# Moving the loads of the transposed h from SyncE's DMA queue to GpSimd's in a two-layer hybrid encoder

## What is computed

```
x = x + 0.5 * swiglu(rmsnorm(x, ffn1_norm), ffn1_w_in, ffn1_w_out)      # D_FF = 2816
h = rmsnorm(x, mix_norm);  p = h @ w_mix_in
out_a = spatial gating over 128-position chunks of p's first 1024 columns
out_b = windowed attention, 8 q heads and 2 kv heads of 64, relative bias rel_bias[bucket], sink
x = x + concat(out_a, out_b) @ w_mix_out
x = x + 0.5 * swiglu(rmsnorm(x, ffn2_norm), ffn2_w_in, ffn2_w_out)
```

## Time and profile before

| | us |
|---|---|
| median of 3 runs | 897.25 |
| lowest, highest | 891.78, 897.42 |
| the profiled execution | 896.2 |
| its span, first to last instruction | 894.4 |

### The profile page before, as it was taken

How to read it: one execution, slowest core, us unless ns; L and a number is a source line. 1 busy time by engine, 2 the same in 40 slices (tenths; PEclk the granted TensorE clock), 3 DMA queues, 4 the chain that set the end, 5 groups by cost and what they waited for, 6 DMA issues and landing times.

```text
span 894.4 us, 11077 instructions
## 1 busy us (share of the span) xinstructions
PE 875.7 (98%) x4118; PEld 715.9 (80%) x4118; DVE 709.5 (79%) x857; ACT 507.0 (57%) x554; POOL 63.8 (7%) x123
## 2 busy tenths in 40 slices
PE   9998999899999999999999999998999999999998
PEld 8886878788788778788887788887877887788887
DVE  6796868667978798878687889775889788989773
ACT  6555637447956466466354664562678573655550
POOL 4200000012101000000010000000111010000000
PEclk9998999999999999999999999999999999999999
DMA  9758677894086858666857587687822878667651
GB/s 316 260 177 263 210 251 247 208 300 157 1 264 210 279 184 286 221 195 248 275 166 242 187 297 248 193 274 236 232 93 71 259 238 273 207 234 227 220 200 48
DMA packets 138469, 194.51 MB, mean 217 GB/s; under 512 B 9796, under 2 KB 94600, under 8 KB 138416
## 3 DMA queue, kind: packets, MB, share of 16 engines
q1 hardware_dynamic: 136432, 189.17, 65.2%
q0 software_dynamic: 1808, 4.49, 2.5%
q10 hardware_dynamic: 176, 0.14, 0.0%
HBM read 179.61 MB, written 14.16 MB: 217 GB/s over the span
## 4 chain that ended last, share of the span: by engine, by line
PE 66%; DVE 17%; DMA 8%; ACT 4%; issue 2%; SPq 2%; ACTq 0%; DVEq 0%
DVE w_lo L1176 7%; PE U L1729 6%; PE U L1732 6%; PE U L1730 6%; PE C L1729 5%; PE C L1730 5%; PE C L1732 5%; PE TR L1729 5%; PE TR L1732 5%; PE TR L1730 5%; PE D L1729 4%; PE D L1730 4%; PE D L1732 4%; DMA gv<-h_rows 4%; DMA h_rows<-qs 3%
## 5 line engine op out<-in xcount | busy, mean ns | idle before, releaser
L1176 DVE TENSOR_TENSOR w_lo<-raw,w_hi 128x2048 fp32r<-128x2048 f32 (+1 forms) x182 | 401.8, 2236 | 47.7 <-ACT w_hi L793 47.2
L793 ACT ACTIVATE w_hi<-raw 128x2048 fp32r<-128x2048 f32 (+1 forms) x178 | 331.7, 1892 | 139.1 <-DVE raw L1201 59.5
L1729 PE MATMUL U<-w_hi,xT 128*128 128x512 f32 (+1 forms) x384 | 147.7, 385 | 0.3 <-DVE xT L1354 0.3
L1730 PE MATMUL U<-w_lo,xT 128*128 128x512 f32 (+1 forms) x384 | 146.2, 381 | 0.0
L1732 PE MATMUL U<-w_hi,xT 128*128 128x512 f32 (+1 forms) x384 | 146.1, 380 | 0.0
L1729 PE MATMUL TR<-w_hi,xT 128*128 128x512 f32 x224 | 87.4, 390 | 0.0
L1732 PE MATMUL TR<-w_hi,xT 128*128 128x512 f32 x224 | 87.2, 389 | 0.0
L1730 PE MATMUL TR<-w_lo,xT 128*128 128x512 f32 x224 | 87.1, 389 | 0.0
L1729 PEld LDWEIGHTS U<-w_hi,xT 128*128 128x128 f32 x384 | 72.2, 188 | 15.6 <-issue 0.8
L1729 PE MATMUL C<-w_hi,hT_hi 128*128 128x512 f32 x176 | 71.7, 408 | 12.3 <-DVE hT_lo L1268 12.3
L1732 PEld LDWEIGHTS U<-w_hi,xT 128*128 128x128 f32 x384 | 72.2, 188 | 13.9
(11 more groups left out here) (210 smaller groups left out, 1238.8 us busy)
## 6 DMA issues: line engine op xcount, KB each, us to landing
raw<-in_ffn_w_in_dram SPq DMA_DIRECT2D x168, 512.0 KB, 5.3
raw<-in_ffn_w_out_dram SPq DMA_DIRECT2D x88, 512.0 KB, 5.5
raw<-in_w_mix_in_dram SPq DMA_DIRECT2D x28, 512.0 KB, 9.5
raw<-in_w_mix_out_dram SPq DMA_DIRECT2D x16, 512.0 KB, 4.4
h_rows<-qs SPq DMA_DIRECT2D x31, 256.0 KB, 2.3
gv<-h_rows SPq DMA_DIRECT2D x124, 64.0 KB, 3.8
raw<-in_ffn_w_in_dram SPq DMA_DIRECT2D x16, 256.0 KB, 4.9
xc<-bias_rows POOLq DMA_DIRECT2D x16, 192.0 KB, 7.4
```

What stands on the lines that cost most here:

```text
L793: return act.activation(w_hi[:, slot_of(u), cols], raw[:, raw_of(u), cols], ACT.Copy)
L1176: return dve.tensor_tensor(w_lo[:, slot_of(u), cols], raw[:, raw_of(u), cols], w_hi[:, slot_of(u), cols].bitcast(F32), ALU.subtract)
L1729: pe.matmul(out_, x_hi, w_hi[:, slot, c], start=start, stop=False, skip_group_check=reopened)
L1730: pe.matmul(out_, x_hi, w_lo[:, slot, c], start=False, stop=False, skip_group_check=reopened)
```

## The change

- `load_h` and `load_g` are issued by GpSimd, with the same waits, data and semaphores. SyncE issues only the stores and the weights, and no longer waits for the stores' landing.
- On GpSimd's queue, `load_h(0, 1)` and `load_h(0, 2)` stand ahead of the store of the bias rows, which now follows unit (0, "out", 2). In layer 1 the loads for chunks 0, 1 and 2 stand ahead of the `ws` loads. All other loads of a layer's first stage stand behind `ws`, `sgain` and `sinks` and ahead of the `bias` loads; those of the second stage behind that layer's last rsqrt for the mixing part.
- The `bias` loads follow (s, "out", 9), three times (s, "out", 7), four times (s, "out", 8).
- In stages 1 to 3 SyncE issues `load_block(s, 3, "B12")` directly behind `store_h(s, 0)`, and `load_out(s, 1)` behind it; before, `load_out(s, 1)` came first and B12 behind the loads of h.
- ScalarE's `round_h(s, 2)` comes ahead of `made(5, 1)`.

```diff
@@ ffn_weights (SyncE), stages 1 to 3
                     store_h(s, 0)
+                    load_block(s, 3, "B12")
                     load_out(s, 1)
-                    load_h(s, 0)
-                    load_block(s, 3, "B12")
                     store_h(s, 1)
                     load_in(s, 5, 0)
-                    load_h(s, 1)
                     load_block(s, 3, "B22")
                     load_out(s, 2)
                     load_in(s, 5, 1)
                     store_h(s, 2)
-                    load_h(s, 2)
...
@@ gpsimd
+            def load_h(s, c):
+                n = TRIP_ORDER[s, c]
+                pool.wait_ge(h_stored, 16 * n)
+                if n > 1:
+                    pool.wait_ge(hT_lo_done, n_h_rest(n - 1))
+                for g in range(4):
+                    src = ...
+                    pool.dma_start(h_cols[32 * g:32 * g + 32, :]..., src).then_inc(h_loaded, 16)
...
-            pool.wait_ge(units_used, n_used((0, "out", 1)))
+            load_h(0, 1)
+            load_h(0, 2)
+            pool.wait_ge(units_used, n_used((0, "out", 2)))
             pool.dma_start(bias_rows, ...)
             for L in range(DEPTH):
                 if L == 0:
                     pool.wait_ge(bias_stored, 16)
+                else:
+                    load_h(s, 0)
+                    load_h(s, 1)
+                    load_h(s, 2)
                 for j, u in enumerate([(s, "sum", 3, "B11"), (s, "sum", 3, "T2"), (s, "in", 5, 0), (s, "in", 6, 0)]):
                     ...
+                load_h(s, 5)
+                load_g(s, 3)
+                load_h(s, 3)
+                load_h(s, 6)
+                load_h(s, 9)
+                load_g(s, 7)
+                load_h(s, 7)
-                for i, u in enumerate([(s, "sum", 7, "B22"), (s, "sum", 7, "B21"), (s, "sum", 7, "T4"), (s, "in", 10, 0),
-                                       (s, "in", 10, 1), (s, "out", 9), (s, "out", 7), (s, "out", 8)]):
+                for i, u in enumerate([(s, "out", 9), *[(s, "out", 7)] * 3, *[(s, "out", 8)] * 4]):
                     ...
                 inverse_rms(L, 2, 1)
+                for c in (0, 1, 2, 5):
+                    load_h(s + 1, c)
+                load_g(s + 1, 3)
+                for c in (3, 6, 9):
+                    load_h(s + 1, c)
+                load_g(s + 1, 7)
+                load_h(s + 1, 7)
@@ scalar
+                round_h(s, 2)
                 made(5, 1)
-                round_h(s, 2)
```

More of the change, by code:

```diff
@@ L552, in store_h @@
                 sp.dma_start(h_rows[n % 2], h_turns).then_inc(h_stored, 16)
[L554 to L563, removed]
             def store_g(s, c):
@@ L571, in store_g @@
                 sp.dma_start(g_rows, g_turns).then_inc(g_stored, 16)
[L573 to L579, removed]
             def trip_of_x(n):
@@ L640, in ffn_weights @@
                 load_block(s, 7, "B12")
-                load_h(s, 5)
                 store_g(s, 3)
@@ L644, in ffn_weights @@
                 store_h(s, 3)
-                load_g(s, 3)
                 load_block(s, 7, "B22")
-                load_h(s, 3)
                 load_in(s, 9, 0)
@@ L652, in ffn_weights @@
                 load_block(s, 7, "B21")
-                load_h(s, 6)
                 load_in(s, 10, 0)
@@ L660, in ffn_weights @@
                 load_out(s, 10)
-                load_h(s, 9)
                 store_g(s, 7)
                 store_h(s, 7)
-                load_g(s, 7)
-                load_h(s, 7)
                 if after is not None:
@@ L730, in norm, with load_g @@
                       groups).then_inc(rstd_done, 1)
+            def load_h(s, c):
[4 more added lines that the diff above has]
+                for g in range(4):
+                    src = bass.AP(h_rows.tensor, TRIP_ORDER[s, c] % 2 * P * 2 * FC + g * P, [[2 * FC, 32], [32 * 2 * FC, 4], [1, P]])
+                    pool.dma_start(h_cols[32 * g:32 * g + 32, :].rearrange("p (i n) -> p i n", i=4), src
+                                 ).then_inc(h_loaded, 16)
+            def load_g(s, c):
+                pool.wait_ge(g_stored, 16 * TRIP_B_ORDER[s, c])
+                for g in range(4):
+                    src = bass.AP(g_rows.tensor, g * P, [[2 * FC, 32], [32 * 2 * FC, 4], [1, P]])
+                    pool.dma_start(g_cols[32 * g:32 * g + 32, :].rearrange("p (i n) -> p i n", i=4), src
+                                 ).then_inc(g_loaded, 16)
             inverse_rms(0, 0, 0)
```

## The result

The changed kernel takes 928.3 us (median of 4 executions, 925.9 to 933.1), the kernel before 897.3 (4, 891.8 to 899.1): ratio 1.036, 95% interval 1.030 to 1.042. It is slower by 31 us where the prediction had 5 us less, and it lies outside the range of 883 to 904. The profiled execution of after took 925.9 (span 924.1, mean granted clock 0.985; before 894.4 and 0.994).

A forecast was written before the change was run, and what follows sets the result against it. TensorE, busy 98% of the span, bounds the kernel, so only its few gaps can be won. Terms -6.3 - 7.2 - 2.2 - 1.1 + 8.0 + 0 + 3.5 = -5.3 us: 896.2 to 890.9, median 892.0; range 883 to 904.

The forecast's parts named there:

- Chunk 2 of stage 0, and chunk 9: Gaps and clock: -6.3 us at chunk 2 of stage 0, -7.2 us at chunk 9 of stages 0 and 2.
- Chunk 5 of stages 0 and 2, the new wait: h(5)'s loads wait behind the last ws load on GpSimd: stall 2.6 us, +8.0 us for both stages.
- Chunk 0 of stages 1 to 3: TensorE's gap 1.5 us, three times 4.6 us as before, so 0; bounds -3.5 and +13.
- L4: Time from the fourth load's issue to landing: about 4.0 us at chunk 0, about 5.8 us at pair 7.
- first rival: GpSimd's loads pass the weights: pair 7 costs 0, chunk 0 -3.5 more; total -13.3 us, median 884; chance 0.15.
- landings of 7 behind weights: GpSimd's h loads were to land in 4 to 6 us behind weights; 3 or 7 would make the prediction wrong.
- Pair 7: SyncE, let go, puts mix weights ahead of the loads: stall 1.75 us, +3.5 us for stages 0 and 2; others 0.
- Chunk 2 of stages 1 to 3 and pair 3: Rounding first gives -2.2 us at chunk 2; GpSimd issuing g's loads gives -1.1 us at pair 3, stage 1.
- Held back B12: At chunk 0 of stages 1 to 3, SyncE's loads of h held back B12 before; no size given.
- the second: Under a saturated queue four GpSimd loads land late, L4 6 at chunk 0: +12.9 us, median 910; chance 0.12.
- The third: TensorE's gaps close but VectorE and ScalarE show them elsewhere: gains halved (+3), median 900; chance 0.12.
- The fourth: VectorE starves descriptors: each of 31 trips 2.25 us later, some 11 in the open: +20 us, median 917; chance 0.03.

The follow-up runs named there:

- Experiment 1: The run of e1_others: kernel before with only the bias-row, bias-load and rounding edits: 880.1 us, ratio 0.980.
- e5_order: Changed kernel with only the order out(1), then B12 restored as in the kernel before, nothing held: 930.3 us, ratio 1.037.
- f_pool_issued: f_pool, but SyncE issues B12 only when GpSimd has issued the four loads of h(0): 892.8 us, ratio 0.997.
- f_pool_landed: f_pool, but SyncE issues B12 only when the four loads of h(0) have landed: 880.3 us, ratio 0.983.
- f_act: f_pool, but ScalarE issues the loads of h(0) on its own queue, ahead of round_h(0): 898.2 us, ratio 1.004.
- e1_others: Kernel before with only the bias rows and bias loads moved and round_h(s, 2) first; all h and g loads stay on SyncE: 880.1 us, ratio 0.980.
- g_landed: Changed kernel with h(5)'s loads ahead of the last ws load and SyncE stopping at each old place until loads have landed: 881.6 us, ratio 0.984.
- f_pool: e1_others, but GpSimd issues the loads of h(0) in stages 1 to 3 and SyncE goes on without a wait: 897.7 us, ratio 1.001.
- g_best: e1_others with load_h(s, 0) ahead of load_out(s, 1) and load_h(s, 3) ahead of load_block(s, 7, B22), all on SyncE: 877.5 us, ratio 0.979.

## Why the prediction was wrong

- **Chunk 2 of stage 0, and chunk 9: right.** -6.3 and -7.2 against -6.5 and -6.8. Experiment 1 shows that they didn't need the new queue.
- **Chunk 5 of stages 0 and 2, the new wait: right.** +8.0 against +9.0 in the trace and +9.9 alone; the gaps were 3.78 and 3.33 us where 2.6 was worked out.
- **Chunk 0 of stages 1 to 3: the step that failed.** The relation (gap = L4 - 2.46) held within 0.3 us: 6.66 gives 4.2 where 4.5 was seen, 7.67 gives 5.2 where 5.4 was. What failed is the term L4: 4.0, worked out from "some 1.2 MB ahead", against 6.7 to 7.7. The bytes were too few: SyncE's queue moved 1.97 MB between the fourth issue and the landing. But the right bytes would not have saved it: e5_order moved 1.30 MB there and landed at 6.8 us. The sentence that led to it was "So a GpSimd load stands behind what SyncE has issued". From a stretch in which GpSimd's queue moved nothing I took a single line in order of issue, in which a load pays only for what stands ahead. The window right behind it, in which SyncE's queue had 58.5% and GpSimd's 53.8%, showed the two sharing; the prediction saw this under its first rival and left it out of the sum. f_pool_issued and f_pool_landed differ only in whether B12 runs beside the loads, and by 12.5 us. The prediction's own sign of being wrong, landings of 7 behind weights, came.
- **Pair 7: half right.** That SyncE let go would put weights beside the loads was seen, for stages 0 and 2; it was sized by the weights ahead (L4 5.8, +3.5) and set to nothing in stage 1. The landings took 7.4, 6.6 and 7.4 us in stages 0, 1 and 2. It costs 12.1 in the trace and 12.8 alone.
- **Chunk 2 of stages 1 to 3 and pair 3:** the small gains came in stages 1 and 2 of chunk 2 (-0.8 and -0.7); chunk 2 of stage 3 and pair 3 lost 5.3 and 2.9. The prediction gave h(3) over 1 us of slack; its loads landed 6.9 and 7.2 us behind the fourth issue in stages 1 and 3, where they had taken 4.6 in stage 1. At chunk 2 of stage 3 the loads landed after 5.6 us beside weights, behind GpSimd's pause of 1.35 us.
- **Held back B12:** the prediction noted that before, the loads "held back B12", and gave this no value. B12 behind the loads in the same queue went with a landing of 3.6 us; about as much of it issued around them from another queue, with 5.9 (f_pool_issued).

Of the rivals, the second, with 0.12, had the right place and the fall of the clock behind it. It spoke of GpSimd loads under a saturated queue; the condition is right (with B12 held away the landing fell to 2.8 to 3.7 us), but f_act shows that they needn't be GpSimd's, and its L4 of 6 was still short. Its 910 left out stage 1 of pair 7. The first, that GpSimd's loads pass the weights, is wrong in the sum: they do get packets in among them, and still land last. The third, that the gains show up again as waits elsewhere, is refuted by e1_others: the terms that it times were worth 15.7 us in the sum and gave 17. The fourth, a trip 2.25 us later for each of 31, finds no such cost in g_landed, where the 39 trips' issues lie beside a VectorE busy 81%. In after, GpSimd's 124 issues of h took (shortest, median, longest in ns):
```profile
L709 POOL DMA_DIRECT2D gv<-h_rows x124: 548/548/675, 45.5 to 898.9; - x124
```
The Trainium skill, SBUF — State Buffer, section SBUF: two separate sides, by which VectorE's two-port instructions hold off GpSimd's writing of descriptors, spoke against the change; this row shows at most 0.13 us of it on one issue. The pause of 1.35 us between two issues isn't in the row; VectorE was making low parts of weights through all of it, and whether that held GpSimd no run tells.

On packets, the Trainium skill, DMA: Bandwidth & Descriptors, section Queues, rings and completion order, says that a DMA engine takes turns between the queues that have work. The traces agree in that both queues are served in one stretch (15.5% beside 76.2% above), but the shares are far from equal, and for 3.8 us of f_pool GpSimd's had none. What I drew from it, that the loads would pass the weights, doesn't follow: taking turns also lets weights issued later go ahead of part of the loads, and a trip ends with its last packet. The same page, section Issuing engines are not separate DMA queues, says that issuing from several engines saves only the time of issue; the 48 us show that it can also cost the order.

## What to carry to other kernels

In this kernel the queue that the small urgent loads shared with the bulk behind them protected them: what was issued later waited. Moved to another queue they had to share with that bulk. Holding the bulk's issuer until they had been issued gave back 5 of the 17.6 us, holding it until they had landed gave back all, and no version with the loads moved was faster than the one that left them. Before moving transfers off a queue, list what the freed engine will issue around them, behind as well as ahead; and where an edit bundles moves with reorderings, time the reorderings by themselves first: here they alone gave 17 us, and the move took away 48.

## What the runs showed of the hardware that was not expected

- Four loads of 64 KB on GpSimd's queue, and equally on ScalarE's, take 5.9 to 7.5 us from the fourth issue beside 1 MB or more of SyncE's weights, and 2.8 to 3.7 with only weights issued earlier; within SyncE's own queue 3.9 to 4.8 with 1 MB ahead and 1 MB behind, and 2.0 with none directly ahead (g_best).
- In such a stretch the queue of the loads had 15.5 to 15.7% of the 16 engines for all of their 0.25 MB, SyncE's 76 to 88%.
- GpSimd's four issues take 2.2 to 2.3 us against SyncE's 1.75, and with nothing else in the way no cost can be told for the three trips of chunk 0: 880.3 against 880.1, ratios 0.983 and 0.980 with intervals that overlap.
- In f_pool, after gaps of 5.0 and 5.3 us, TensorE's granted clock was 0.69 and 0.70 over the next 5.4 and 5.8 us, a mean between its levels of 2.4 and 1.2 GHz; with gaps of up to 2.1 us in the version of 880.1 us the profiled mean stayed 1.0. Length alone doesn't tell: in before the clock stayed full behind a gap of 2.79 us, in the changed kernel it was 0.70 over the 5.6 us behind one of 2.51.
